# The start of a block kernel: part of a small matrix product moved to TensorE, x taken in two transfers, one copy left out

## The reference

```python
mod = c @ w_ada + b_ada                       # c: 1 x 1024, w_ada: 1024 x 3072
shift, scale, gate = split(mod, 3)
h = rms_norm(x, g_pre) * (1.0 + scale) + shift   # x: 512 x 1024
proj = h @ w_in                               # queries, keys, values, gates ...
kc = silu(flat(blocks(kc_raw) + pe) @ w1) @ w2   # compression: blocks of 32, stride 16; same for values
```

## Time and profile before

| | |
|---|---|
| median of three runs | 1599.93 us (1599.43, 1608.46, 1599.93) |
| the profiled execution | 1602.58 us, span 1600.8 us |
| TensorE matmul busy | 1532.8 us (96%), 9576 instructions |
| VectorE, ScalarE, GpSimd busy | 754.8, 531.5, 596.9 us |
| TensorE's mean granted clock | 0.979 of 2.4 GHz |
| HBM traffic | 86 GB/s over the span |

### The profile page before, as it was taken

The page is one execution under the profiler, slowest core; times in us unless marked ns, Lnnn a source line. Parts: engine busy times, 40 slices in busy tenths (PEclk is TensorE's granted clock), DMA queues, the critical chain, the costliest instruction groups (busy, mean ns, idle before and its releaser), DMA issues.

```text
span 1600.8 us, 24864 instructions
## 1 busy us (share of the span) xinstructions
PE 1532.8 (96%) x9576; PEld 1368.3 (85%) x9576; DVE 754.8 (47%) x1538; ACT 531.5 (33%) x939; POOL 596.9 (37%) x481
## 2 busy tenths in 40 slices
PE   3999999999999899999999999899999999999996
PEld 2688888888777899999999999798798889879885
DVE  6845666566567733332332321423623642362355
ACT  4444444343333433223223232232323332332332
POOL 5463232221254253444435345143433243334331
PEclk9999999999999999999999999899999999999998
DMA  9232111111234122222222222122131122212111
GB/s 369 93 121 77 54 52 52 52 52 53 105 108 182 53 84 95 85 105 79 79 105 79 82 103 79 53 79 80 53 105 52 62 95 79 79 52 95 63 53 53
DMA packets 22468, 138.18 MB, mean 86 GB/s; under 512 B 3216, under 2 KB 3216, under 8 KB 6544
## 3 DMA queue, kind: packets, MB, share of 16 engines
q1 hardware_dynamic: 18320, 127.93, 22.3%
q10 hardware_dynamic: 4096, 9.53, 1.7%
HBM read 135.36 MB, written 2.10 MB: 86 GB/s over the span
## 4 chain that ended last, share of the span: by engine, by line
PE 61%; issue 23%; POOL 11%; DVE 3%; ACT 1%; DMA 1%; POOLq 0%; DVEq 0%; ACTq 0%
PE lin L383 54%; POOL w_lo L324 10%; PE aux L915 3%; PE aux L890 2%; DMA residual<-x_t 1%; DVE square_sum L409 1%; PE aux L873 0%; POOL residual L356 0%; PE aux L417 0%; PE aux L899 0%; PE aux L445 0%; PE aux L840 0%; PE aux L875 0%; DVE residual L1803 0%; ACT squares L1244 0%
## 5 line engine op out<-in xcount | busy, mean ns | idle before, releaser
L324 POOL TENSOR_TENSOR w_lo<-w_raw,w_hi 128x512 fp32r<-128x512 f32 x448 | 583.4, 1334 | 974.1 <-ACT w_hi L371 974.1
L383 PE MATMUL lin<-x_hi,w_hi 128*128 128x512 f32 (+2 forms) x2056 | 562.4, 328 | 18.4 <-DVE x_lo L1303 7.2
L383 PE MATMUL lin<-x_lo,w_hi 128*128 128x512 f32 (+2 forms) x2056 | 556.3, 325 | 0.0
L383 PE MATMUL lin<-x_hi,w_lo 128*128 128x512 f32 (+2 forms) x2056 | 552.9, 323 | 0.0
L383 PEld LDWEIGHTS lin<-x_hi,w_hi 128*128 128x128 f32 x2056 | 345.4, 191 | 50.4 <-issue 8.5
L383 PEld LDWEIGHTS lin<-x_hi,w_lo 128*128 128x128 f32 x2056 | 344.5, 191 | 30.8
L383 PEld LDWEIGHTS lin<-x_lo,w_hi 128*128 128x128 f32 x2056 | 345.2, 191 | 26.9
L371 ACT ACTIVATE w_hi<-w_raw 128x1024 fp32r<-128x1024 f32 x224 | 223.9, 1049 | 175.3 <-PE lin L383 169.4
L1033 ACT ACTIVATE prob<-prob,neg_max 128x31 f32<-128x31 f32 (+6 forms) x128 | 60.2, 471 | 133.7 <-DVE neg_max L1430 133.7
L1568 DVE TENSOR_TENSOR conv_in<-conv_c_gate,lin 128x272 f32<-128x272 f32 (+1 forms) x30 | 11.6, 427 | 191.2 <-PE lin L383 191.2
L383 PE MATMUL lin<-mix,w_hi 128*128 128x512 f32 x256 | 80.9, 397 | 2.4 <-DVE mix L1749 1.9
(11 more groups left out here) (331 smaller groups left out, 1959.8 us busy)
## 6 DMA issues: line engine op xcount, KB each, us to landing
w_raw<-wstream SPq DMA_DIRECT2D x112, 1024.0 KB, 4.7
ada_shift_scale<-w_ada SPq DMA_DIRECT2D x8, 1024.0 KB, 20.7
ada_gate<-w_ada_gate ACTq DMA_DIRECT2D x4, 1024.0 KB, 5.0
residual<-x_t SPq DMA_DIRECT2D x1, 2048.0 KB, 10.4
residual<-x_t ACTq DMA_DIRECT2D x1, 2048.0 KB, 8.7
out_t<-residual ACTq DMA_DIRECT2D x8, 256.0 KB, 2.1
small_inputs<-smalls ACTq DMA_DIRECT2D x1, 537.0 KB, 3.9
c_on_lanes<-c_row ACTq DMA_DIRECT2D x1, 512.0 KB, 6.7
```

Source lines behind the costliest of these rows:

```text
L324: eng.tensor_tensor(wlo[h][:, cols], raw[h][:, cols], whi[h][:, cols].bitcast(F32), ALU.subtract).then_inc(s_lo, 1)
L383: ins = t.matmul(o, w[half][:, c0:c0 + P], x(k, t0, cnt), start=(n == 0), stop=(n == 3 * kts - 1))
```

## The change

x comes in two transfers of five and three tiles. The c_row transfer moves from ScalarE's queue to SP's, ahead of w_ada's fifth block; chunk 1's goes one block earlier. ScalarE takes a Sqrt of a constant first, then the squares, in four buffers. For k = 0 to 3 shift and scale are computed on TensorE: shift_and_scale(k) is 16 f32 matmuls whose weights are 128x128 pieces of the w_ada block and whose moving operand is one column of c, into two columns of lin[1]; the first call stands between the sum and the spread of the root, three follow behind it. VectorE only adds the bias and multiplies (shift_and_scale_out). For k = 4 to 7 it goes on as before, after c has been copied to lin[1]. VectorE multiplies x's first three tiles by the root from PSUM and copies the root to rstd; GpSimd multiplies the other five. compression_input reads the banks of chunk 0's result, and cmp_kv goes. Waits in the attention count on VectorE's own semaphore in place of s_opart, and s_gate_sum is now s_ada_sum. The host lays w_ada's first four blocks out by input rows.

```diff
+N_ADA_PE, X_FIRST, X_DVE = 4, 5, 3
...
-        cmp_kv = sb("cmp_kv", [2, T1], stack=stage_c_right, side="right")
...
-            eng.dma_start(res[:, :, META:T2], x_t).then_inc(s_x, 16)
+            eng.dma_start(res[:, 0:X_FIRST, META:T2], x_t[:, 0:X_FIRST, :]).then_inc(s_x, 16)
+            eng.dma_start(res[:, X_FIRST:, META:T2], x_t[:, X_FIRST:, :]).then_inc(s_x_rest, 16)
             eng.dma_start(raw[0][:], wstream[0, :, :]).then_inc(raw_full[0], 16)
             for k in range(N_ADA):
-                if k == 4:
+                if k == N_ADA_PE:
+                    eng.dma_start(c_rows[:], c_row).then_inc(s_c, 16)
+                if k == N_ADA_PE - 1:
                     eng.dma_start(raw[1][:], wstream[1, :, :]).then_inc(raw_full[1], 16)
                 eng.dma_start(ada_w[:, k, :], w_ada[k, :, :]).then_inc(s_ada[k], 16)
...
-            low_parts(0, 0)
+            def x_hat(k):
+                eng.tensor_tensor(res[:, k, META:T2], res[:, k, META:T2], rstd[:, 0:T1], ALU.mult).then_inc(s_xhat, 1)
+            low_parts(0, 0, pieces=[0, 1])
+            low_parts(0, 0, pieces=[2])
+            eng.wait_ge(s_xhat, X_DVE)
             eng.wait_ge(s_rstd, 1)
-            for k in range(KD):
-                eng.tensor_tensor(res[:, k, META:T2], res[:, k, META:T2], rstd[:, 0:T1], ALU.mult).then_inc(s_xhat, 1)
-                if 2 <= k < 2 + PIECES:
-                    low_parts(1, 1, pieces=[k - 2])
+            x_hat(3)
+            x_hat(4)
+            low_parts(0, 0, pieces=[3])
+            x_hat(5)
+            low_parts(1, 1, pieces=[0])
+            x_hat(6)
+            low_parts(1, 1, pieces=[1])
+            x_hat(7)
+            low_parts(1, 1, pieces=[2, 3])
...
+        def squares_of(k):
+            return (sq, tmp)[k // 2 % 2][:, k % 2, 0:T1]
...
+            def shift_and_scale(k):
+                eng.wait_ge(s_ada[k], 16)
+                if k >= 2:
+                    eng.wait_ge(s_mod, k - 1)
+                for x in range(2):
+                    for r in range(KD):
+                        ins = eng.matmul(lin[1][:, k % 2, x:x + 1], ada_w[:, k, D * x + P * r:D * x + P * r + P], c_in[:, r:r + 1],
+                                         start=(r == 0), stop=(r == KD - 1))
+                ins.then_inc(s_ada_sum, 1)
             eng.wait_ge(s_const, 21)
+            eng.wait_ge(s_small, 16)
             norm_total_pe(eng, n0, TB1, KD)
-            norm_spread_pe(eng, n0, TB1)
+            shift_and_scale(0)
+            norm_spread_pe(eng, n0, TB1, bank=0)
+            for k in range(1, N_ADA_PE):
+                shift_and_scale(k)
...
                         if g:
                             eng.wait_ge(s_gate_th, 1)
-                        eng.wait_ge(s_proj_out, g + 1)
+                        else:
+                            eng.wait_ge(s_cin, 1)
                     else:
-                        eng.wait_ge(s_proj_out, 2 * (at - 1) + g + 1)
+                        eng.wait_ge(s_proj_out, 2 * (at - 2) + g + 1)
...
-                eng.wait_ge(s_proj_out, (4, 6, 8)[s])
+                eng.wait_ge(s_proj_out, (2, 4, 6)[s])
+                if s == 0:
+                    eng.wait_ge(s_cin, 2)
...
-            eng.dma_start(c_rows[:], c_row).then_inc(s_c, 16)
+            eng.wait_ge(s_const, 21)
+            act(rcol[:, 0:1], eps[:], ACT.Sqrt)
             eng.wait_ge(s_x, 16)
             for k in range(KD):
-                if k >= 2:
-                    eng.wait_ge(n0.added, max(k - 2, 1))
-                act(sq[:, k % 2, 0:T1], res[:, k, META:T2], ACT.Square).then_inc(n0.squared, 1)
+                if k == X_FIRST:
+                    eng.wait_ge(s_x_rest, 16)
+                if k >= 4:
+                    eng.wait_ge(n0.added, max(k - 4, 1))
+                act(squares_of(k), res[:, k, META:T2], ACT.Square).then_inc(n0.squared, 1)
             chunk_lands_and_splits(eng, 0)
-            eng.wait_ge(s_const, 21)
             norm_root_act(eng, n0, TB1, D)
-            eng.wait_ge(n0.spread, 1)
-            act(rstd[:, 0:T1], aux[2][:], ACT.Copy).then_inc(s_rstd, 1)
             eng.dma_start(res[:, :, 0:META], meta_t).then_inc(s_x, 16)
-            eng.wait_ge(s_rstd, 1)
             for k in range(KD):
                 eng.wait_ge(s_xhat, k + 1)
...
                 x_mod = dict(scale=scale_c[:, k:k + 1], bias=mod[:, k:k + 1])
                 act(aux[2 + k % 2][:], res[:, k, META:T2], ACT.Identity, **x_mod)
                 act(xhi[:, k, 0:T1], res[:, k, META:T2], ACT.Identity, **x_mod).then_inc(s_xhi, 1)
-                if k == 1:
+                if k == 2:
...
-            eng.wait_ge(s_c, 16)
-            for b in range(2):
-                own.up(copy(c_spread[:, 512 * b:512 * b + 512], c_rows[:, 512 * b:512 * b + 512]))
-            for k in range(KD):
-                norm_add_dve(eng, n0, k, T1, KD)
+            eng.wait_ge(n0.squared, 2)
+            tt(ssum[:, 0:T1], squares_of(0), squares_of(1), ALU.add).then_inc(n0.added, 1)
+            for k in range(2, KD):
+                eng.wait_ge(n0.squared, k + 1)
+                eng.wait_ge(n0.added, k - 1)
+                tt(ssum[:, 0:T1], ssum[:, 0:T1], squares_of(k), ALU.add).then_inc(n0.added, 1)
+            def shift_and_scale_out(k):
+                eng.wait_ge(s_ada_sum, k + 1)
+                own.up(ts(mod[:, k:k + 1], lin[1][:, k % 2, 0:1], bada[:, k:k + 1], None, ALU.add))
+                ts(scale_c[:, k:k + 1], lin[1][:, k % 2, 1:2], mod[:, 2 * KD + k:2 * KD + k + 1], gpre[:, k:k + 1],
+                   ALU.add, ALU.mult).then_inc(s_mod, 1)
...
-            shift_and_scale(0)
             norm_invert_dve(eng, n0, TB1)
-            shift_and_scale(1)
-            shift_and_scale(2)
-            low(0)
-            low(1)
-            for k in range(3, KD):
-                shift_and_scale(k)
-                low(k - 1)
-            low(KD - 1)
+            shift_and_scale_out(0)
+            eng.wait_ge(n0.spread, 1)
+            for k in range(X_DVE):
+                tt(res[:, k, META:T2], res[:, k, META:T2], aux[0][:], ALU.mult).then_inc(s_xhat, 1)
+                if k == 0:
+                    copy(rstd[:, 0:T1], aux[0][:]).then_inc(s_rstd, 1)
+            for k in range(1, N_ADA_PE):
+                shift_and_scale_out(k)
+            eng.wait_ge(s_mod, N_ADA_PE)
+            eng.wait_ge(s_c, 16)
+            for b in range(2):
+                own.up(copy(c_spread[:, 512 * b:512 * b + 512], c_rows[:, 512 * b:512 * b + 512]))
+            own.settle()
+            for k in range(KD):
+                low(k)
+                if k + 1 in range(N_ADA_PE - 1, KD - 1):
+                    shift_and_scale(k + 2)
...
-                        ins = copy(values[:, VALUES[c], :] if c else cmp_kv[:, g, :], proj_bank(c, g))
+                        ins = copy(values[:, VALUES[c], :], proj_bank(c, g))
...
-                eng.wait_ge(s_proj_out, 2)
+                    eng.wait_ge(s_chunk, START["proj"] + 1)
+                else:
+                    eng.wait_ge(s_proj, 1)
                 for g in range(2):
                     gs = slice(g * DH, (g + 1) * DH)
-                    rows_of = cmp_kv[gs, src, :].rearrange("p (j a r) -> p r a j", a=8, r=2)
+                    rows_of = proj_bank(0, src)[gs, :].rearrange("p (j a r) -> p r a j", a=8, r=2)
...
-            copy_out(0)
             compression_input(0)
             copy_out(1)
             compression_input(1)
...
-                    ts(o_b, o[:, 3 * DH:4 * DH], coef[:, 3:4], None, ALU.mult).then_inc(s_opart, 1)
-                    eng.wait_ge(s_opart, ii * 16 + (2 * s + 1))
-                    stt(o_a, o[:, DH:2 * DH], coef[:, 1:2], o_a, ALU.mult, ALU.add).then_inc(s_opart, 1)
-                    eng.wait_ge(s_opart, ii * 16 + (2 * s + 2))
+                    own.up(ts(o_b, o[:, 3 * DH:4 * DH], coef[:, 3:4], None, ALU.mult))
+                    own.settle()
```

More of the change, by code:

```diff
@@ L110, in build @@
         s_hi, s_lo, s_chunk = sem("chunk_hi"), sem("chunk_lo"), sem("chunk_done")
-        s_small, s_x, s_const, s_out = sem("small_in"), sem("x_in"), sem("const"), sem("out_stored")
+        s_small, s_x, s_x_rest, s_const, s_out = sem("small_in"), sem("x_in"), sem("x_rest_in"), sem("const"), sem("out_stored")
         s_ada = [sem(f"ada{i}") for i in range(N_ADA)]
@@ L129, in build @@
         s_pt, s_pt_act, s_pt_dve = sem("prob_turned"), sem("prob_out_act"), sem("prob_out_dve")
-        s_recip, s_pv, s_opart, s_o = sem("reciprocals"), sem("weighted"), sem("output_parts"), sem("outputs")
+        s_recip, s_pv, s_o = sem("reciprocals"), sem("weighted"), sem("outputs")
         s_oT, s_oT_out = sem("outputs_turned"), sem("outputs_turned_out")
@@ L135, in build @@
         s_wo, s_wo_out, s_y, s_yhi, s_ylo = sem("wo_tile"), sem("wo_out"), sem("y"), sem("y_hi_done"), sem("y_lo_done")
-        s_out_tile, s_out_out, s_gate_sum, s_gate_tot = (sem(n) for n in ("out_tile", "out_out", "ada_gate_summed", "ada_gate_total"))
```

(23 more changed lines are left out.)

## The result

The changed kernel takes 1618.38 us (median of 6 runs, 1614.30 to 1623.38) against 1602.95 us for the kernel before (6 runs beside it, 1599.43 to 1608.46): ratio 1.0097, 95% interval 1.0076 to 1.0118. It is 1% slower. The profiled execution took 1614.30 us with a span of 1612.5, 11.7 more than the span before.

A forecast was written before the change was run, and what follows sets the result against it. TensorE's chain was taken as the bound, after a start paced by VectorE. Compress ending 13.1 later, 12.6 after the keys, put 1602.58 at 1615.2, a median of 1612.5; own range 1608 to 1618, outer 1604 to 1621.

The forecast's parts named there:

- The rate that decides: One-column records of the four TensorE calls run at the low clock, pitch 0.213: 6.8 us a call, 144 records in 30.7.
- Rival (a): The clock rises under TensorE's one-column stream: 16.9 us instead of 30.7, 1.2 faster, 1598.7 us; chance 0.10.
- Rival (b): The clock rises late, for example after the second TensorE call: 6.8 us less than forecast, 1605.7; chance 0.05.
- Rival (c): Accumulating one-column records don't overlap and take 0.35 us each, not 0.213: 18 us more, 1630; chance 0.05.
- x and the sum: At the start, x in two transfers lands at 8.0 and TensorE's sum starts at 15.6, 3.1 us earlier.
- the block: GpSimd's w_lo starts under the last add of squares and holds it; sum taken at 15.6, against 14.8 from pitches alone.
- Rival (d): x's two parts share the queue and land together near 10: 2 us more, 1614.5, within the own range.
- What queues on VectorE: x_lo(0) stands behind all four results and two copies, 48.1 for 28.1; TensorE's work to the gates' end shifts by 17.8.
- Compression inputs: Eight adds from PSUM at 0.6 us each (bounds 0.59 and 1.46); the 3.0 wait and the clock's fall behind it go.
- The sum: All parts together: 12.6 us more, 1615.2 for the profiled execution and a median of 1612.5, 0.8% slower.
- the keys' wait: TensorE's wait of about 0.5 us for the keys' low parts at 84.78 goes, through the earlier second compression input.
- At nothing: Parts put at no cost: the attention's waits, the gate sums' renamed semaphore, GpSimd's later w_lo piece, chunk 2's later transfer.

The follow-up runs named there:

- experiment 3: The changed kernel with ten 512-wide f32 matmuls, result unused, in TensorE's idle time ahead of the sum: 1621.05 us in one run.
- experiment 5: The kernel before with only the compression inputs read from their PSUM banks, copies gone: 1597.17 us, ratio 0.9964 to the kernel before.
- experiment 6: experiment 1 with VectorE's three x products given back to GpSimd: 1597.23 us, ratio 0.9967 to the kernel before.
- experiment 7: experiment 6 with GpSimd's low parts of chunk 0 waiting for the last add of squares: 1591.97 us, ratio 0.9936 to the kernel before.
- experiment 1: The changed kernel with the four calls back on VectorE and c's rows again on ScalarE's queue: 1596.35 us, ratio 0.9947 to the kernel before.

## Why the prediction was right

The forecast of 1612.5 us, 0.8% slower, stands against 1618.38 and 1.0%: inside 1604 to 1621, and 0.4 beyond my own range of 1608 to 1618. The mechanism is the one that was forecast.

**The rate that decides.** Right, and for the reason given. 144 records took 16.35 to 47.21, 30.9 us, where I had 30.7. Rival (a) is refuted: the clock never rose in 27 us of the stream, nor did it stay up when dense work had lifted it ahead (experiment 3). Rival (b) with it. Rival (c) is refuted by the pitch: accumulating records follow each other at 0.213. The rule of the Trainium skill (TensorE: Matmul & The Clock Gate, Part 1) that sustained matmul time warms the array does not hold for this stream; it holds for the 512-wide work behind it, at 0.41 after 4.0 us (3.1 to 6.1 across the runs here).

**x and the sum.** x came at 8.67, not 8.0, for a reason that no run settles. My rate of 413 GB/s isn't what the earlier trace rows shows (424), and what I had land together did not: before, the small inputs were there at 4.69 and c's rows at 7.96. But 0.67 is also about what runs with the same transfers differ by: the first square is at 11.21 before and at 10.68 in experiment 5, at 9.49, 9.59 and 10.11 in experiments 6, 7 and 1. Seven adds with GpSimd on the last took 7.68 us from the first square; I had 7.6 with the block and 6.9 without it, and experiment 7 shows the two cases apart, 7.69 and 6.80. Rival (d) did not occur, but two thirds of a microsecond of its direction did.

**What queues on VectorE.** Right in each step, 0.7 to 0.9 us late from the start on: x_lo(0) 49.00 for 48.1, x_lo(2) 51.37 for 50.5, x_lo(3) 54.68 for 53.9, x_lo(6) 64.60 for 63.9, and the gates' end 80.8 for 80.1. The two copies of c's rows stood on the path, as forecast (47.68 to 48.97).

**Compression inputs.** The direction was right, the size not: an add takes 0.41 us (pitch 0.38), below my lower bound of 0.59. I had taken the row without GpSimd as the best case, but one operand in PSUM is faster still. GpSimd starts at 71.10, beside the last adds, and does not slow them: with one SBUF input they are not blocked, as the Trainium skill says (SBUF — State Buffer, Who interferes with whom). The low part has both inputs in SBUF and GpSimd beside it; it took 1.79 us for my 1.2 (the second one, also beside GpSimd, 1.30), which used up half of the 1.0 us of slack that I had. That the wait and the fall of the clock behind it would both go was right; experiment 5 shows it alone.

**The sum.** +13.8 at project(3) for my +13.1, and the keys' wait gone. The profiled pair differs by 11.7 only. Adding up one-microsecond stretches from 66 us on with a granted clock below 1.00, without the last ten, the kernel before has 58.0 us at the low level and the changed one 51.2. Of the 58.0, 3.4 are the fall at the compression (from 66.2 on), ahead of project(3) and so in the +13.8 already; that leaves 54.6 against 51.2. The kernel before went from 1599.12 us at a mean clock of 0.981 to 1609.23 at 0.974, so a clock lost costs about its own time (0.007 of 1600 is 11.2 us, for 10.1), and a microsecond at half the clock 0.45 to 0.5. That gives back 1.5 to 1.7 us in this pair. 13.8 less 0.4 less that is 11.7 to 11.9, for 11.7 measured. So the profiled 1614.30 came within 0.9 of my 1615.2 partly by luck: 0.7 more from x's landing, 1.6 less from the places of the low clock, which I had only as 3 either way. The median against 1599.93 was forecast at 1612.5. Of the 5.9 us to the measured 1618.38, 3.0 are that the kernel before itself measures 1602.95 in six runs, 0.7 is x's landing, and 2.2 are not accounted for.

**At nothing.** The table load, the semaphores and chunk 2's later transfer cost nothing that any row of the changed kernel shows. (The early Sqrt is worth something once the calls are gone: experiment 6.) Between 54 and 112 us none of TensorE's waits reaches half a microsecond.

## What to carry to other kernels

Before moving a small product to TensorE, look in the trace for the same form (here one-column f32 matmuls, 128x128 weights each) and read its pitch at both clock levels; here it ran at the low one, but for the first 2 us in the kernel with dense work ahead of it. Compare that price with the idle time it fills, not with what it saves elsewhere: here 6.8 us a call replaced a 2.7 us round on an engine whose other work then waited. And take a change apart: x in two transfers, the early Sqrt and the inputs from their banks were gains (the four square buffers came with the first two, and no run has them apart), the calls on TensorE and the products on VectorE were not, and without these, with one wait that keeps GpSimd off the last adds, the kernel is 0.6% faster than before instead of 1% slower.

## What the runs showed of the hardware

A mixture in which 512-wide matmuls took 0.57 of every 1.28 us did not lift the clock in 40 us (durations 0.77 and 0.71 to the end), and in one run did not hold it once it was up. 512-wide work alone lifted it each time, but not after one fixed time: the first matmul at 0.39 to 0.41 came 3.1 us after the first one before (28.95 to 32.08), 4.0 in the changed kernel, 5.7 with wide work mixed in (61.62 to 67.30) and 6.1 in experiment 1 (31.25 to 37.33).

In these traces the granted clock column reads 1.00 from the start until the clock has first been up and fallen, whatever the durations say (0.77 us for a 512-wide matmul at 49.84 in a stretch with 1.00). In the kernels with dense work ahead, the same stream at the same durations reads 0.50. The column shows falls, and its first reading has to be checked against a duration. The mean clock of such a run is lower for that reason too (0.964 with dense work ahead).

A strided f32 add of 64x248 takes 0.41 us with one operand in PSUM (0.38 to the next start), beside GpSimd too; with both in SBUF it takes 0.59 alone and 1.46 beside GpSimd. The median of all 16 of them in the changed kernel:

```profile
L1408 DVE TENSOR_TENSOR cmp_in<-lin,small_inputs x16: 399/410/421, 69.2 to 87.1; 64x248 f32<-64x248 f32 x16
```

Runs of one kernel differ by the clock they are granted: the six of the changed kernel go from 1614.30 us at a mean of 0.981 to 1623.38 at 0.975.
